# Expert values: 88 of 128 blocks gathered by row, 40 read in order and multiplied by a one-hot weight matrix; all key rows first

## The chip, the cores and the metric

The kernel runs on one core of a Trainium2 chip. The metric is the time of one execution on the device in microseconds. The profile shows the engines PE (TensorE), DVE (VectorE), ACT (ScalarE), POOL (GpSimd) and SP (SyncE), and the 16 DMA engines that all of them use.

## The reference, cut to what matters

Two transformer blocks run over 256 tokens of width 2048. Everything up to the second block's mixer is left out here: the change does not touch it. The last layer is a product-key expert layer:

```python
q = (xt @ wq).reshape(T, 8, 2, 128)
s1 = einsum('thd,nd->thn', q[:, :, 0], subkeys[0])
s2 = einsum('thd,nd->thn', q[:, :, 1], subkeys[1])
v1, i1 = top_k(s1, 16)
v2, i2 = top_k(s2, 16)
cand = (v1[..., :, None] + v2[..., None, :]).reshape(T, 8, 256)
sc, ci = top_k(cand, 16)
e1 = take_along_axis(i1, ci // 16, axis=-1)
e2 = take_along_axis(i2, ci % 16, axis=-1)
idx = e1 * 128 + e2
gate = softmax(sc, axis=-1)
h = gelu(einsum('cd,chkd->chk', xc, u[idx]))
out = einsum('chk,chkd->cd', gate * h, v[idx])
```

Each token picks 16 experts in each of 8 heads, 128 picks in all. An expert has a row of `u` and a row of `v`, each 2048 f32 numbers (8 KB). There are 16384 experts: 128 blocks (by `e1`) of 128 rows (by `e2`), 1 MB a block. The result is added to x, and a last RMS norm with a gain gives the output.

## The kernel before, in words

The 256 tokens are two tiles of 128, one token per partition. The picks of one head for one tile are a group `g` of 16 (tile `g // 8`, head `g % 8`); there are 16 groups. POOL fetches rows by indirect DMA, `gather` (L620): one DMA brings, for pick `r` of group `g`, one row per partition, 128 rows of 8 KB. Eight slots of 1 MB in SBUF (four in `arena`, four in `proj`) take the rows in turn: row number n goes to slot `n % 8`, and POOL waits until the slot's earlier row was used (`free0` to `free7`). The order is 16 u rows of group 0, and from then on one u row of group `g + 1` and one v row of group `g` in turn (`U_ROW`, `V_ROW`).

DVE does the choosing and the dot products. `choose_sides` takes the best 16 of each side's 128 scores, `choose_sums` the best 16 of the 256 sums, and `experts_of` (L2670) turns them into row numbers. `dot_row` (L2712) multiplies a u row with x and sums. ACT's gelu and DVE's `weigh` (L2729) make the 16 weights of a group. Three of four v rows are added by PE: ACT makes a diagonal matrix of the weights (L1068) and PE multiplies it with the row, four matmuls of 512 columns into PSUM (L1899). The others are added by DVE: `add_row` (L2722) is one SCALAR_TENSOR_TENSOR over 2048 columns, then a wait for itself and a semaphore raised for the slot. `link` is a helper that raises DVE's own semaphore and waits for it.

In between PE still works out the queries of heads 4 to 7 (`ask_part`, L1873), for which SP loads blocks of `peer_wq`; ACT copies their scores out (`take_head`). SP then loads the final gain (L399, a broadcast load of 128 rows of 8 KB). `join` (L2744) adds PE's sums to x and `last_mean` and `last_norm` do the final norm: for tile 0 at groups 8 to 10, beside the gathers of tile 1, and for tile 1 at the end. ACT takes the squares' sums (L1012) and roots (L1014), and writes half of tile 1's output.

## Time and profile before

| | |
|---|---|
| median of 3 runs | 3221.64 us (3220.44 to 3223.31) |
| span of the profiled execution | 3220.0 us |
| busy, share of the span | PE 84%, DVE 62%, POOL 29%, ACT 14% |
| DMA | 922.82 MB, mean 287 GB/s |
| expert stage in the span | from 1890.84 us on |

The span runs from the first to the last instruction of the profiled execution. No time of its own is listed for that execution outside the profile; the median of the runs is 1.6 us above its span, and that is taken for what lies around it. Busy shares are means over stages with different limits, so the stage that the change touches is read by itself.

### The profile page before, as it was taken

To read this page: it belongs to the slowest core of one execution; us is meant where nothing else is said; L and a number is where in the kernel's file an instruction comes from. 1 tells how busy PE (TensorE), PEld (TensorE's weight loads), DVE (VectorE), ACT (ScalarE), POOL (GpSimd) and SP (SyncE) were. 2 spreads that over 40 slices of the span, in tenths; PEclk is the share of its full clock that TensorE was granted. 3 is DMA by queue.
4 is the path that set the end of the run, shared out by engine and by line. 5 is a ranking of instruction groups with operands and counts; after the bars stand their busy time and mean duration, and the time that the engine had idled before them with its cause. 6 is when DMAs were issued, how large, how long until landed. Compare 5 with 4: busy or idle time off the path is not lost.

```text
span 3220.0 us, 26360 instructions
## 1 busy us (share of the span) xinstructions
PE 2717.7 (84%) x9138; PEld 1612.9 (50%) x9138; DVE 1985.4 (62%) x3009; ACT 441.8 (14%) x1072; POOL 926.9 (29%) x713
## 2 busy tenths in 40 slices
PE   5999998999999999999999996878666666666666
PEld 2444666488888884445568473434322222222222
DVE  6555466288666655543037668667766676776655
ACT  1000133211111010002037021000000001000001
POOL 2111200000000000000014036556566566666664
PEclk9999989999999999999999997889887888888888
DMA  9999541467555545555440569999999999999998
GB/s 377 359 397 399 201 134 40 170 222 256 162 169 169 169 157 183 174 179 164 131 157 1 198 254 417 419 419 422 422 422 421 422 414 400 422 422 422 422 422 355
DMA packets 250245, 922.82 MB, mean 287 GB/s; under 512 B 16732, under 2 KB 44580, under 8 KB 183844
## 3 DMA queue, kind: packets, MB, share of 16 engines
q0 software_dynamic: 99840, 637.57, 48.3%
q1 hardware_dynamic: 149893, 283.38, 26.4%
q8 instruction: 54, 0.88, 0.1%
q10 hardware_dynamic: 416, 0.66, 0.1%
q14 instruction: 42, 0.34, 0.0%
HBM read 918.35 MB, written 8.44 MB: 288 GB/s over the span
## 4 chain that ended last, share of the span: by engine, by line
PE 56%; DMA 22%; DVE 11%; POOL 5%; issue 4%; ACT 2%; POOLq 0%; SPq 0%; DVEq 0%; ACTq 0%
PE ps L1505 16%; DMA arena<-in_peer_v,proj 13%; PE ps L1133 12%; PE ps L1551 8%; PE ps L1899 7%; DMA proj<-in_peer_v,proj 5%; PE ps L1749 3%; DMA arena<-in_peer_u,proj 3%; POOL proj L625 3%; DMA arena<-in_w_mod 2%; PE ps L1175 2%; PE ps L1259 1%; DVE arena L2716 1%; PE ps L1272 1%; DVE proj L2716 1%
## 5 line engine op out<-in xcount | busy, mean ns | idle before, releaser
L1899 PE MATMUL ps<-arena,gates 128*128 128x512 f32 x516 | 364.9, 872 | 368.9 <-DMA arena<-in_peer_v,proj 255.1
L1899 PE MATMUL ps<-proj,gates 128*128 128x512 f32 x992 | 449.4, 598 | 39.2 <-DMA proj<-in_peer_v,proj 38.9
L1899 PEld LDWEIGHTS ps<-arena,gates 128*128 128x128 f32 x516 | 142.0, 289 | 585.0 <-issue 455.4
L2716 DVE CUSTOM_DVE_ANT_0 proj<-proj,yT 128x2048 f32<-128x2048 f32 x128 | 291.8, 2291 | 229.5 <-DMA proj<-in_peer_u,proj 228.9
L1133 PE MATMUL ps<-ring,hT 128*128 128x512 f32 (+3 forms) x960 | 373.5, 551 | 1.8 <-DVE arena L2427 1.8
L2716 DVE CUSTOM_DVE_ANT_0 arena<-arena,yT 128x2048 f32<-128x2048 f32 x128 | 292.3, 2292 | 119.9 <-DMA arena<-in_peer_u,proj 116.4
L1899 PEld LDWEIGHTS ps<-proj,gates 128*128 128x128 f32 x992 | 184.7, 190 | 289.0 <-issue 287.8
L1133 PEld LDWEIGHTS ps<-ring,hT 128*128 128x128 f32 x960 | 180.1, 192 | 191.9 <-issue 165.6
L625 POOL DMA_INDIRECT arena<-in_peer_u,proj x128 | 200.1, 1563 | 234.2 <-PE ps L1817 119.2
L625 POOL DMA_INDIRECT proj<-in_peer_u,proj x128 | 230.0, 1797 | 100.2 <-DVE proj L2716 57.2
L1505 PE MATMUL ps<-arena,yT 128*128 128x256 f32 x1056 | 242.3, 379 | 0.0
L595 POOL COPY proj<-proj 128x256 f32 (+1 forms) x16 | 5.9, 395 | 814.5 <-DVE proj L2481 814.5
L625 POOL DMA_INDIRECT proj<-in_peer_v,proj x128 | 188.1, 1470 | 135.0 <-PE ps L1899 117.3
L625 POOL DMA_INDIRECT arena<-in_peer_v,proj x128 | 172.3, 1346 | 160.9 <-PE ps L1899 135.6
L1505 PEld LDWEIGHTS ps<-arena,yT 128*128 128x128 f32 x1056 | 199.0, 190 | 26.2
L1969 DVE SCALAR_TENSOR_TENSOR arena<-arena,c_col 128x1024 f32<-128x1024 f32 (+1 forms) x120 | 154.2, 1285 | 76.4 <-DMA arena<-in_w_mod 73.8
L1505 PE MATMUL ps<-ring,hT 128*128 128x256 f32 x704 | 166.4, 379 | 1.2 <-ACT hT L665 1.2
L2725 DVE SCALAR_TENSOR_TENSOR x<-arena,proj,x 128x2048 f32<-128x2048 f32 x63 | 148.1, 2350 | 15.4 <-DMA arena<-in_peer_v,proj 15.4
L2315 DVE TENSOR_TENSOR arena<-ring 128x512 f32<-128x512 f32 x88 | 60.9, 692 | 148.3 <-PE ps L1505 147.9
L1505 PEld LDWEIGHTS ps<-ring,hT 128*128 128x128 f32 x704 | 133.7, 190 | 19.9 <-ACT hT L665 1.4
L542 POOL DMA_DIRECT2D arena<-in_w_mod x80 | 56.8, 710 | 280.9 <-PE ps L1133 129.2
L591 POOL DMA_DIRECT2D proj<-in_w_mod x16 | 11.3, 708 | 384.4 <-DVE gates L1969 200.2
(500 smaller groups left out, 3727.9 us busy)
## 6 DMA issues: line engine op xcount, KB each, us to landing
arena<-in_w_mod POOLq DMA_DIRECT2D x80, 1024.0 KB
ring<-in_ffn_w_gate SPq DMA_DIRECT2D x44, 1024.0 KB, 5.2
ring<-in_ffn_w_up SPq DMA_DIRECT2D x44, 1024.0 KB, 5.2
ring<-in_ffn_w_down SPq DMA_DIRECT2D x88, 512.0 KB, 5.2
ring<-in_w_in SPq DMA_DIRECT2D x40, 1024.0 KB, 8.7
ring<-in_w_out SPq DMA_DIRECT2D x16, 1024.0 KB, 5.2
proj<-in_w_mod POOLq DMA_DIRECT2D x16, 1024.0 KB
ring<-in_w_out SPq DMA_DIRECT2D x32, 512.0 KB, 4.8
```

Of the source, the lines that this page charges most:

```text
L542: pool_eng.dma_start(mod["ring"][:, j % 4], w_mod[:, 2 * j:2 * j + 2, cols]).then_inc(sem(f"mod_slot{j % 4}"), 16)
L625: pool_eng.indirect_dma_start(row_slots[n % ROWS], None, table, bass.IndirectOffsetOnAxis(expert[:, 0, TOP * g + r:TOP * g + r + 1], 0))\
L1133: ins = pe.matmul(ps[:, 2 * (b % 2) + t, 0:w], lhs[:, KS * (order[s] if between and b == 0 else s) + k, P * t:P * (t + 1)], ring[:, s, k, ...
L1175: ins = pe.matmul(ps[:, 2 * b + t, 0:FIRST], hT[:, KS * q + k, P * t:P * (t + 1)], ring[:, b, k, 0:FIRST], start=(q == 0 and k == 0), stop ...
L1505: ins = pe.matmul(up_ps(m, UP_PLACE[name], 1), tokens(j), weights[:, j, :], start=first and name in UP_FIRST, stop=(q == SLOTS - 1 and j = ...
L1551: return pe.matmul(ps[:, bank[name], :], lhs, rhs, start=(k == 0), stop=(k == HALF_K - 1))
L1749: return pe.matmul(ps[:, bank[name], :], lhs, rhs, start=(k == 0), stop=(k == OUT2_HALF - 1))
L1899: ins = pe.matmul(ps[:, 4 * t + b, :], diag[:, j, :], row_slots[n % ROWS][:, NB * b:NB * (b + 1)], start=(h == 0 and j == 0), stop=(h == H ...
L1969: ins = vec.scalar_tensor_tensor(out=to, in0=w, scalar=c, in1=to, op0=ALU.mult, op1=ALU.add)
L2315: link(vec.tensor_tensor(w["S1"], a21, a22, ALU.add), "w_sums", wait=False)
L2716: vec.tensor_tensor_reduce(slot, slot, xs[:, g // HEADS], 1.0, 0.0, ALU.mult, ALU.add, peer["h16"][:, 0, r:r + 1]).then_inc(sem(f"free{n % ...
L2725: link(vec.scalar_tensor_tensor(out=x[:, t], in0=row_slots[n % ROWS], scalar=peer["weight"][:, 0, TOP * g + r:TOP * g + r + 1], in1=x[:, t ...
```

## The change

The value blocks 88 to 127 (`TILES = 40`) are no longer gathered. Their rows are read in order, a block of 128 rows at a time, and multiplied on PE by a weight matrix [128 experts of the block, 128 tokens] for each block and tile. The gathers of v get a bound (`bounds_check=LAST_GATHERED`): rows past block 87 are skipped, the slot keeps what it held, and the weight for them is set to 0 (`near`).

The reference, run on its own inputs, puts 29.9% of tile 0's picks and 31.4% of tile 1's into these 40 blocks.

The weight matrices are built from one-hot rows. ACT and PE turn the picks (`side1` = e1, `side2` = e2, and the weights) so that one column holds the 128 picks of a token. For four tokens at a time (`GROUP`), DVE compares e2 with 0..127 (`hot2`, 4 x 128 columns) and e1 with 88..127 (`hot1`, 4 x 40 columns), POOL multiplies `hot1` by the weights, PE multiplies the two (one matmul of 40 columns per token), and ACT copies the result into `W_HOME`. A tile takes 32 such steps.

The order changes. All u rows go first; tile 0's 128 v rows are mixed in from group 2 on, 9 to a group of 16 u rows, and PE adds all of them. Tile 0's weight matrices are built beside groups 9 to 14. After the last u row come tile 1's 128 v rows, all of them added by DVE. Tile 1's weight matrices are built first, four steps ahead of each of DVE's first eight additions. SP loads the first three blocks once all experts are known; the other 37, and the final gain ahead of them, wait until all weight matrices are built and then for PE's release of a buffer of three. Tile 0's `join` and norm move to the end, ahead of tile 1's. The final gain moves into `arena`; `vrows` and `vcols` become one tensor; the table of constants gets 128 columns of iota for 16.

```diff
+    U_ORDER = [(g, r) for g in range(GS) for r in range(TOP)]
+    V_AFTER = {}
+    for g in range(2, GS):
+        for r in range(TOP):
+            if (9 * r) // TOP != (9 * (r + 1)) // TOP or (g >= GS - 2 and r == 0):
+                V_AFTER[g, r] = len(V_AFTER)
+    assert len(V_AFTER) == PICKS
+    U_ROW, V_ROW = {}, {}
+    for g, r in U_ORDER:
+        U_ROW[g, r] = len(U_ROW) + len(V_ROW)
+        if (g, r) in V_AFTER:
+            V_ROW[V_AFTER[g, r]] = len(U_ROW) + len(V_ROW)
+    for v in range(PICKS, 2 * PICKS):
+        V_ROW[v] = 2 * PICKS + v
...
+    TILES = 40
+    GATHERED = P - TILES
+    LAST_GATHERED = P * GATHERED - 1
+    GROUP = 4
+    GROUPS = P // GROUP
+    SPREAD_AT = {TOP * (HEADS + 1) + 3 * i: i for i in range(GROUPS)}
+    PE_LAG, POOL_LAG = 4, 8
+    TAIL = 4
+    spread_at = lambda g, r, lag=0: SPREAD_AT.get(TOP * g + r - lag)
+    HOT = GROUP * (P + TILES)
...
+    v_tiles = (tab[:, TAB.shape[1] - D:], gates[:, 0, :], arena[:, D:2 * D])
+    NV = len(v_tiles)
+    v_in = lambda e: at(f"slot{e % NV}", 16 * (BLK["wq"] + 3 + e // NV + 1))
+    v_used = lambda n: at("unit_used", SLOTS * (BLK["wq"] + 4) + n)
...
-        sp.wait_ge(*at("unit_used", SLOTS * (BLK["wq"] + 4)))
-        load("norm_in", out_gain, a["final_norm_2"].partition_broadcast(P))
+        sp.wait_ge(*at("experts", GS + 1))
+        for e in range(TILES):
+            if e == NV:
+                sp.wait_ge(*at("w_built", 2 * GROUPS))
+                load("norm_in", out_gain, a["final_norm_2"].partition_broadcast(P))
+            if e >= NV:
+                sp.wait_ge(*v_used(e - NV + 1))
+            sp.dma_start(v_tiles[e % NV], a["peer_v_2"][P * (GATHERED + e):P * (GATHERED + e + 1), :]).then_inc(sem(f"slot{e % NV}"), 16)
...
+        def gather_v(v):
+            n = V_ROW[v]
+            row_wait(n)
+            pool_eng.indirect_dma_start(row_slots[n % ROWS], None, a["peer_v_2"], bass.IndirectOffsetOnAxis(expert[:, 0, v:v + 1], 0),
+                                        bounds_check=LAST_GATHERED, oob_is_err=False).then_inc(sem(f"row{n % ROWS}"), 16)
+        def hot_weights(i):
+            t, j = divmod(i, GROUPS)
+            pool_eng.wait_ge(*at("pick_out", 3 if t else 1))
+            pool_eng.wait_ge(*at("hot", i + 1))
+            pool_eng.tensor_tensor(hot1(i), hot1(i), pick_T(t, 2)[:, GROUP * j:GROUP * (j + 1)].unsqueeze(2).to_broadcast([P, GROUP, TILES]), ALU.mult)\
+                    .then_inc(sem("hot_weights"), 1)
...
+        for g, r in U_ORDER:
+            if g == 0 and r % FEW == 0:
                 pool_eng.wait_ge(*at("experts", r // FEW + 1))
+            if g and r == 0:
+                pool_eng.wait_ge(*at("experts", g + 2))
+            gather_u(g, r)
+            if (g, r) in V_AFTER:
+                gather_v(V_AFTER[g, r])
+            if spread_at(g, r, POOL_LAG) is not None:
+                hot_weights(spread_at(g, r, POOL_LAG))
+        for v in range(PICKS):
+            for i in range(TAIL * (v - ROWS), TAIL * (v - ROWS + 1)):
+                if 0 <= i < GROUPS:
+                    hot_weights(GROUPS + i)
+            gather_v(PICKS + v)
...
+        def diag_out(v):
+            act.wait_ge(*at("weights", v // TOP + 1))
+            if v >= NDIAG:
+                act.wait_ge(*row_free(V_ROW[v - NDIAG]))
+            act.activation(diag[:, v % NDIAG, :], ident, ACT.Copy, scale=peer["near"][:, 0, v:v + 1]).then_inc(sem("diag_out"), 1)
+        def picks_out(n, lo, hi):
+            act.wait_ge(*at("pick_turned", n + 1))
+            t = min(n, 1)
+            act.copy(vboth[:, 3 * t + lo:3 * t + hi, :], ps[:, 6, P * lo:P * hi].rearrange("p (k m) -> p k m", m=P)).then_inc(sem("pick_out"), 1)
+        def spread_out(i):
+            t, j = divmod(i, GROUPS)
+            act.wait_ge(*at("w_built", i + 1))
+            built = ps[:, w_bank(i), 0:GROUP * TILES].rearrange("p (j e) -> p e j", j=GROUP)
+            for lo, n, home in W_HOME[t]:
+                ins = act.copy(home[:, :, GROUP * j:GROUP * (j + 1)], built[:, lo:lo + n, :])
+            ins.then_inc(sem("w_out"), 1)
...
+        def add_row(v):
+            n = V_ROW[v]
+            pe.wait_ge(*at("diag_out", v + 1))
+            pe.wait_ge(*row_in(n))
+            for b in range(SLOTS):
+                ins = pe.matmul(ps[:, b, :], diag[:, v % NDIAG, :], row_slots[n % ROWS][:, NB * b:NB * (b + 1)], start=(v == 0), stop=False, skip_group_check=True)
+            ins.then_inc(sem(f"free{n % ROWS}"), 1)
...
+        def spread(i):
+            pe.wait_ge(*at("hot_weights", i + 1))
+            if i >= 2:
+                pe.wait_ge(*at("w_out", i - 1))
+            for j in range(GROUP):
+                ins = pe.matmul(ps[:, w_bank(i), TILES * j:TILES * (j + 1)], hot2(i)[:, j, :], hot1(i)[:, j, :], start=True, stop=True)
+            ins.then_inc(sem("w_built"), 1)
...
+        def sum_values(t, e, banks):
+            pe.wait_ge(*v_in(e))
+            for b in banks:
+                ins = pe.matmul(ps[:, 4 * t + b, :], spread_weights(t, e), v_tiles[e % NV][:, NB * b:NB * (b + 1)],
+                                start=(t == 1 and e == 0), stop=(e == TILES - 1), skip_group_check=True)
+            return ins
+        pe.wait_ge(*at("weights", GS))
+        turn_picks(1, (2,))
+        for i in range(GROUPS):
+            spread(GROUPS + i)
+            early = i - (GROUPS - SLOTS * NV)
+            if early >= 0:
+                sum_values(0, early // SLOTS, (early % SLOTS,))
+        pe.wait_ge(*at("w_out", 2 * GROUPS))
+        for e in range(TILES - NV):
+            if e >= NV:
+                sum_values(0, e, range(SLOTS))
+            sum_values(1, e, range(SLOTS)).then_inc(sem("unit_used"), 1)
+        for t, banks in ((0, range(SLOTS)), (1, (2, 3)), (1, (0, 1))):
+            for e in range(TILES - NV, TILES):
+                ins = sum_values(t, e, banks)
+            ins.then_inc(sem("values_done"), 1)
...
-        def add_row(g, r):
-            t, n = g // HEADS, V_ROW(g, r)
+        def add_row(v):
+            n = V_ROW[v]
             vec.wait_ge(*row_in(n))
-            link(vec.scalar_tensor_tensor(out=x[:, t], in0=row_slots[n % ROWS], scalar=peer["weight"][:, 0, TOP * g + r:TOP * g + r + 1], in1=x[:, t],
-                                          op0=ALU.mult, op1=ALU.add))
+            link(vec.scalar_tensor_tensor(out=x[:, 1], in0=row_slots[n % ROWS], scalar=peer["near"][:, 0, v:v + 1], in1=x[:, 1], op0=ALU.mult, op1=ALU.add))
             vec.sem_inc(sem(f"free{n % ROWS}"), 1)
+        def hot_sides(i):
+            t, j = divmod(i, GROUPS)
+            vec.wait_ge(*at("pick_out", t + 1))
+            if i >= 3:
+                vec.wait_ge(*at("w_built", i - 2))
+            place = lambda k, n: pick_T(t, k)[:, GROUP * j:GROUP * (j + 1)].unsqueeze(2).to_broadcast([P, GROUP, n])
+            vec.tensor_tensor(hot2(i), place(1, P), tb("iota").unsqueeze(1).to_broadcast([P, GROUP, P]), ALU.is_equal)
+            vec.tensor_tensor(hot1(i), place(0, TILES), tb("iota")[:, GATHERED:P].unsqueeze(1).to_broadcast([P, GROUP, TILES]), ALU.is_equal).then_inc(sem("hot"), 1)
...
+            link(vec.scalar_tensor_tensor(out=w, in0=w, scalar=total, in1=peer["h"][:, 0, TOP * g:TOP * (g + 1)], op0=ALU.mult, op1=ALU.mult))
+            picks = slice(TOP * g, TOP * (g + 1))
+            link(vec.scalar_tensor_tensor(out=peer["near"][:, 0, picks], in0=peer["side1"][:, 0, picks], scalar=float(GATHERED), in1=w, op0=ALU.is_lt, op1=ALU.mult), "weights")
...
+            if 0 < g < GS - 1:
+                choose_sides(g + 1)
             for r in range(TOP):
+                dot_row(g, r)
+                if (g, r) == (0, 3):
+                    choose_sides(1)
+                if r == (3 if g else 7) and g + 1 < GS:
+                    choose_sums(g + 1)
+                if g and r == 5:
+                    weigh(g - 1)
+                if spread_at(g, r) is not None:
+                    hot_sides(spread_at(g, r))
+            dots_done(g)
+        for i in range(GROUPS, GROUPS + 2):
+            hot_sides(i)
+        weigh(GS - 1)
+        for v in range(PICKS):
+            for i in range(TAIL * v, TAIL * (v + 1)):
+                if 2 <= i < GROUPS:
+                    hot_sides(GROUPS + i)
+            add_row(PICKS + v)
+        join(0)
+        last_mean(0)
+        last_norm(0)
```

## Rows read from the trace of the kernel before

**Rows 1.** The page's 40 slices (part 2), and POOL's first gather in the timeline.

```profile
DMA  9999541467555545555440569999999999999998
...
1890.84 1.04 POOL L625 DMA_INDIRECT arena<-in_peer_u,proj  x1 [119.17 <-PE ps L1817]
```

**Rows 2.** Windows of 80 us; x counts instructions; then clock, DMA share, rate.

```profile
core 0: us, PE busy (x) PEld busy (x) DVE busy (x) ACT busy (x) POOL busy (x), PEclk, DMA share, GB/s
...
2520.00:2600.00 80.00, 51.37 (x96) 20.62 (x94) 55.98 (x78) 6.79 (x17) 47.54 (x33) 0.83 1.01 421
...
2680.00:2760.00 80.00, 51.04 (x95) 20.82 (x94) 55.60 (x78) 10.45 (x23) 50.75 (x33) 0.83 0.98 401
```

**Rows 3.** The page's costliest groups: busy us, mean ns, idle before and its releaser.

```profile
L2716 DVE CUSTOM_DVE_ANT_0 proj<-proj,yT 128x2048 f32<-128x2048 f32 x128 | 291.8, 2291 | 229.5 <-DMA proj<-in_peer_u,proj 228.9
...
L2725 DVE SCALAR_TENSOR_TENSOR x<-arena,proj,x 128x2048 f32<-128x2048 f32 x63 | 148.1, 2350 | 15.4 <-DMA arena<-in_peer_v,proj 15.4
```

**Rows 4.** DVE's timeline at the end: start, duration, instruction, idle before.

```profile
3188.14 2.35 DVE L2725 SCALAR_TENSOR_TENSOR x<-arena,proj,x 128x2048 f32<-128x2048 f32 x1 [2.62 <-DMA arena<-in_peer_v,proj]
3193.11 2.35 DVE L2725 SCALAR_TENSOR_TENSOR x<-arena,proj,x 128x2048 f32<-128x2048 f32 x1 [2.62 <-DMA arena<-in_peer_v,proj]
...
3207.98 1.28 DVE L2741 SCALAR_TENSOR_TENSOR x<-arena,proj,x 128x1024 f32<-128x1024 f32 x1 [2.57 <-DMA arena<-in_peer_v,proj]
```

**Rows 5.** DVE's timeline: choosing sides and weighing; choosing sums, then dots in a row.

```profile
1954.11 0.17 DVE L2720 COPY proj<-proj 128x16 f32<-128x16 f32 x1
...
1958.02 2.29 DVE L2716 CUSTOM_DVE_ANT_0 arena<-arena,yT 128x2048 f32<-128x2048 f32 x1
...
1980.42 0.42 DVE L2707 TENSOR_TENSOR arena<-arena 128x256 f32<-128x256 f32 x1
...
1987.64 2.29 DVE L2716 CUSTOM_DVE_ANT_0 proj<-proj,yT 128x2048 f32<-128x2048 f32 x1
...
1989.86 2.29 DVE L2716 CUSTOM_DVE_ANT_0 proj<-proj,yT 128x2048 f32<-128x2048 f32 x1
```

**Rows 6.** DVE's two-input operations over 512 and 256 columns.

```profile
L2315 DVE TENSOR_TENSOR arena<-ring 128x512 f32<-128x512 f32 x88 | 60.9, 692 | 148.3 <-PE ps L1505 147.9
...
L2678 DVE TENSOR_TENSOR arena<-arena,tab 128x256 f32<-128x256 f32 x32 | 13.7, 427 | 1.1
```

**Rows 7.** DVE's timeline where such an operation raises a semaphore for another engine.

```profile
1905.43 2.35 DVE L2771 SCALAR_TENSOR_TENSOR yT<-x,stat,arena 128x2048 f32<-128x2048 f32 x1
1907.98 2.29 DVE L2716 CUSTOM_DVE_ANT_0 arena<-arena,yT 128x2048 f32<-128x2048 f32 x1 [0.19 <-DVE yT L2771]
```

**Rows 8.** DMA queues while the final gain loads, 2284 to 2286 us.

```profile
q1 hardware_dynamic: 58, 0.48, 56.8%
q0 software_dynamic: 52, 0.37, 44.4%
```

**Rows 9.** PE among the last gathers: eight matmuls, and the window around them.

```profile
3190.74 3.67 PE L1899 MATMUL ps<-arena,gates 128*128 128x512 f32 x8 [1.30 <-DMA arena<-in_peer_v,proj]
...
3190.00:3200.00 10.00, 7.34 (x16) 2.88 (x16) 4.76 (x3) 0.00 (x0) 2.25 (x2) 1.00 1.01 420
```

**Rows 10.** DVE's timeline from the first join of the end to its last product.

```profile
3209.41 1.22 DVE L2749 TENSOR_TENSOR x<-x,ps 128x1024 f32<-128x1024 f32 x1
...
3214.54 1.28 DVE L2763 SCALAR_TENSOR_TENSOR x<-x,stat,hT 128x1024 f32<-128x1024 f32 x1
```

**Rows 11.** POOL's timeline beside dots in a row and beside idle; window of the whole stage.

```profile
1944.13 1.91 POOL L625 DMA_INDIRECT arena<-in_peer_u,proj  x1 [0.31 <-issue]
1946.34 1.91 POOL L625 DMA_INDIRECT proj<-in_peer_v,proj  x1 [0.30 <-issue]
...
1976.71 0.94 POOL L625 DMA_INDIRECT proj<-in_peer_u,proj  x1 [0.30 <-issue]
1977.96 0.94 POOL L625 DMA_INDIRECT arena<-in_peer_v,proj  x1 [0.30 <-issue]
...
1890.00:3210.00 1320.00, 910.20 (x2109) 424.36 (x2108) 916.08 (x1260) 123.17 (x310) 790.50 (x512) 0.84 1.00 415
```

More of the change, by code:

```diff
@@ L619, in _, with row_wait @@
         head_pair(0, 7, False)
-        def gather(table, g, r, n):
+        def row_wait(n):
             pool_eng.wait_ge(*at(f"free{n % ROWS}", n // ROWS + 1))
@@ L624, in gather, with gather_u @@
                 pool_eng.wait_ge(*at("unit_used", SLOTS * BLK["wq"] + n - 2))
-            pool_eng.indirect_dma_start(row_slots[n % ROWS], None, table, bass.IndirectOffsetOnAxis(expert[:, 0, TOP * g + r:TOP * g + r + 1], 0))\
+        def gather_u(g, r):
+            n = U_ROW[g, r]
+            row_wait(n)
+            pool_eng.indirect_dma_start(row_slots[n % ROWS], None, a["peer_u_2"], bass.IndirectOffsetOnAxis(expert[:, 0, TOP * g + r:TOP * g + r + 1], 0))\
                     .then_inc(sem(f"row{n % ROWS}"), 16)
-        for r in range(TOP):
-            if r % FEW == 0:
-                pool_eng.wait_ge(*at("experts", r // FEW + 1))
-            gather(a["peer_u_2"], 0, r, U_ROW(0, r))
@@ L632, in _ @@
[L632 to L638 removed]
+        def gather_v(v):
+            n = V_ROW[v]
+            row_wait(n)
+            pool_eng.indirect_dma_start(row_slots[n % ROWS], None, a["peer_v_2"], bass.IndirectOffsetOnAxis(expert[:, 0, v:v + 1], 0),
+                                        bounds_check=LAST_GATHERED, oob_is_err=False).then_inc(sem(f"row{n % ROWS}"), 16)
@@ L1033, in take_head, with take_scores @@
             act.copy(peer["q"][:, h % 2], ps[:, pair:pair + 2, 0:T]).then_inc(sem("wq_out"), 1)
+        def take_scores(h):
+            pair = 4 + 2 * (h % 2)
             act.wait_ge(*at("keys_scored", h + 3))
@@ L1057, in _ @@
         for h in range(2, EARLY):
-            take_head(h)
-        best_exp(1)
-        for g in range(GS):
-            act.wait_ge(*at("h_done", g + 1))
-            h = peer["h"][:, 0, TOP * g:TOP * (g + 1)]
-            act.activation(h, h, ACT.Gelu_apprx_tanh).then_inc(sem("h_gelu"), 1)
-            act.wait_ge(*at("weights", g + 1))
-            if g:
-                act.wait_ge(*v_added(g - 1))
-            for j, r in enumerate(by_pe(g)):
-                act.activation(diag[:, j, :], ident, ACT.Copy, scale=peer["weight"][:, 0, TOP * g + r:TOP * g + r + 1]).then_inc(sem("diag_out"), 1)
-            if g == HEADS + 1:
-                last_norm(0)
-            if 0 < g <= HEADS - EARLY:
-                take_head(EARLY + g - 1)
-            if g + 2 < GS:
-                best_exp(g + 2)
+            take_queries(h)
+            take_scores(h)
+        for g, r in U_ORDER:
+            if g and r == 0:
+                row_gelu(g - 1)
+            if (g, r) in V_AFTER:
+                diag_out(V_AFTER[g, r])
+            if (g, r) in TAKE_Q:
+                take_queries(TAKE_Q[g, r])
+            if (g, r) in TAKE_SCORES:
+                take_scores(TAKE_SCORES[g, r])
+            if r == 9 and g + 1 < GS:
+                best_exp(g + 1)
+            if (g, r) == (HEADS, 8):
+                picks_out(0, 0, 3)
+            if (g, r) == (GS - 1, 8):
+                picks_out(1, 0, 2)
+            if spread_at(g, r, PE_LAG) is not None:
+                spread_out(spread_at(g, r, PE_LAG))
+        row_gelu(GS - 1)
+        picks_out(2, 2, 3)
+        for i in range(GROUPS, 2 * GROUPS):
+            spread_out(i)
         act.activation(stat[:, 12:13], stat[:, 30:31], ACT.Sqrt)
+        last_norm(0)
         last_norm(1)
@@ L1887, in _ @@
         score_head(EARLY - 1)
-        for g in range(GS):
-            t, h = g // HEADS, g % HEADS
-            if g == HEADS:
+        def add_row(v):
[5 more added lines that the diff above has]
+            ins.then_inc(sem(f"free{n % ROWS}"), 1)
@@ new lines, in turn_picks @@
+        def turn_picks(t, ks):
+            for k in ks:
+                src = peer[("side1", "side2", "weight")[k]][:, 0, PICKS * t:PICKS * (t + 1)]
+                ins = pe.transpose(ps[:, 6, P * k:P * (k + 1)], src, ident)
+            ins.then_inc(sem("pick_turned"), 1)
+        def spread(i):
[5 more added lines that the diff above has]
+            ins.then_inc(sem("w_built"), 1)
@@ new lines, in _ @@
+                pe.wait_ge(*at("weights", HEADS))
+                turn_picks(0, range(3))
+            if (g, r) == (GS - 1, 8):
+                pe.wait_ge(*at("experts", GS + 1))
+                pe.wait_ge(*at("pick_out", 1))
+                turn_picks(1, range(2))
+            if spread_at(g, r, PE_LAG) is not None:
+                spread(spread_at(g, r, PE_LAG))
+        def sum_values(t, e, banks):
[4 more added lines that the diff above has]
+            return ins
```

140 lines of the change are left out of this document (52 added, 88 removed).

## The prediction

> **What bounds the kernel now.** I read the forty slices of the page first, to find the stage. From slice 25 on the DMA row is full [rows 1]: this is the expert stage, from 1890.8 us, where the first gather is issued, to 3208 us, where the last one lands [rows 1, 4]. Busy time in a window of 80 us, one group's time, shows the DMA at 1.01 of 16 engines and 421 GB/s while DVE is busy for 56 us, PE for 51 and POOL for 48 [rows 2]. So transfers set the pace, and DVE has 24 us in 80 to spare. The groups by line say the same: the dot products' idle time ends on DMA, 229.5 us of it before one of the two groups [rows 3]. The pace itself stands at the end of the timeline: DVE takes every second row there and starts a new one each 4.97 us [rows 4], so one gather of 128 rows of 8 KB costs 2.485 us. 512 of them are 1272 us of the 1317.
>
> **What the change removes.** The reference's own picks, counted, lie in the last 40 blocks for 29.9% of tile 0 and for 31.4% of tile 1. If a skipped row costs nothing, a value gather falls to 0.701 x 2.485 = 1.74 us (tile 0) and 0.686 x 2.485 = 1.70 us (tile 1): 95 + 100 = 195 us of DMA go, and 40 blocks of 1 MB, 99 us, come back. Net 96 us of transfers. The question is how much of that reaches the end, since u rows now come first and DVE alone adds tile 1 (128 additions where it had 67, one of them half a row).
>
> **Stage 1, all u rows and tile 0's values.** Groups 0 and 1 have no values. A group costs DVE 16 dots at a pitch of 2.22 us, 35.5, choosing sides and weighing 3.9, choosing sums 7.2 [rows 5], and the new masked weights, about 0.2, by the other operations of 16 columns (0.17 [rows 5]): 47 us, against 40 of transfers, so DVE sets these two. From group 2 a group moves 16 u rows and 9.14 value rows, 39.8 + 15.9 = 55.7 us, which is above DVE's 47 and, with 5.33 pairs of one-hot compares from group 9 on, above 53. A pair is 512 and 160 columns: 0.69 and 0.33 us, between the rows for 512 and 256 columns [rows 6]. PE's 36 matmuls per group are 16 us at the pitch below: hidden. ACT's diagonals too. The end of the stage, worked out from before: the last landing, 3208, less 128 tile-1 gathers (318), less tile 0's skipped rows (95), less the gain load and tile 0's output (5), less about 8 us by which the windows of the stage fell short of 422 GB/s, half of them in the one where tile 0 was joined, normed and written out (401 GB/s) [rows 2], plus three value blocks that SP loads early (7.5): 2789. **Stage 1 ends at 2797.**
>
> A rule of the Trainium skill bears on the second: DMA: Bandwidth & Descriptors, section The descriptor swizzle, ties four and four partitions to an engine. By it the busiest engine would hold 772 rows and the stage would end 17 us later than even skipping gives; no row here shows which engine a row used.
>
> **Stage 2, the second weight matrix.** DVE's last weights go through ACT, PE and POOL: about 6 us. Then DVE alternates four pairs of compares, 4 x 1.05, with one addition, eight times. An addition is 2.35 us [rows 3] and waits for itself and raises a semaphore; the same pattern left 0.2 us before the next instruction [rows 7], so 2.55. With some waits for POOL and PE, three deep, I take 7.3 a turn, 58 in all; bounds 6.75 (no wait) and 9 (one POOL operation per turn held up by an addition). Together **64 us, to 2861**. Until then only the first three blocks can be loaded, and only eight gathers refill: DMA idles for about half, some 30 us, of what was saved.
>
> **Stage 3, the blocks.** SP's queue then brings 37 blocks and the gain while POOL's brings gathers. The only load of this form beside a full gather queue, the final gain, got 58 packets where the gathers got 52 in the two microseconds in which it ran throughout [rows 8], so each side gets half, and a block takes 4.97 us. PE needs 8 matmuls per block, 3.67 us, and that very rhythm, 8 per 4.97 us, ran at a clock of 1.00, the 2.4 GHz level [rows 9], so PE keeps up and three buffers keep SP's queue full. 38 x 4.97 = **189 us, to 3050**. A gather now takes 2 x 1.70 = 3.41 us, so 55 land, and DVE, which could do 74, starves.
>
> **Stage 4, what is left.** Of 128 rows 8 were added, 8 had landed, 55 came: 57 remain at DVE's 2.55 (their transfers, 1.70, are shorter): **145 us, to 3195**. The order of the two queues thus costs what the skipping gained: first DVE waits for DMA, then DMA for DVE.
>
> **The end.** Before, 10.6 us passed from the first join to the end of the span [rows 10]. Tile 0's join, norm and output were hidden; they now stand ahead of it on DVE: two joins of 1.22, squares and root 2.5, two products of 1.28: 7.6. In all 18 us, **3213**. The profile's span is 3220.0, the median of the runs 3221.6, so 1.6 lies around it: **3215 us**, 0.2% less.
>
> **The rivals.** *DVE stays fed (faster).* If SP's loads get less than half, say 40%, stage 3 takes 38 x 2.485 / 0.4 = 236 us, gathers take 2.84 us, 83 land, 29 remain: 236 + 74 = 310 where the sum has 334, so 3191; with no starving at all DVE's 120 additions, 306, give 3187. For it: a block waits for PE's release, a gather only for DVE. Against: the packets of the gain load.
>
> *POOL becomes the bound (slower).* Where DVE works without a gap, POOL issues one gather per dot, 2.21 us apart; where DVE runs short operations or idles, 1.25 us apart [rows 11]. Stage 1 asks 25.1 gathers and, from group 9 to 14, 5.33 products of a group that should take 55.7 us. That is 1.83 us each: from there this decides, and the mean of the whole stage before was 1.54 + 0.30 = 1.84 (512 gathers in 790 us, and the gap named issue) with DVE busy for some 70% [rows 11]. It will be 85 to 95%. At 2.05 those six groups take 62 us, 38 more, so 3253; at 2.21, 69 more. A bounds check that lengthens the gather adds to it. Against: when DMA sets the pace DVE waits for rows, and in these gaps POOL is fast.
>
> The Trainium skill speaks for this one: GPSIMD Engine Reference, section Key points, says that POOL shares its SBUF interfaces with VectorE and contends with instructions that have two SBUF inputs, as the dots have; the pitch of 2.21 agrees, and by that rule the compares and additions would hold POOL up too.
>
> *Skipping saves nothing (slower).* If a row out of bounds is fetched from a clamped address, stage 1 is 95 us longer; in stage 3 a gather takes 4.97, 38 land, 74 remain, 189 us instead of 145: 3215 + 95 + 44 = 3354. Nothing in this trace speaks for or against, as no gather had a bound; it is the plainest way for the change to fail.
>
> **How the numbers follow.** A measurement here tells 0.2% (6.4 us) from no change. The sum holds with chance 0.52; its own bounds, about -20 (no additions, 6.75 a turn) to +35, spread it as 0.23 faster, 0.15 same, 0.14 slower, likeliest range 3195 to 3250. DVE fed: 0.20, faster. POOL: 0.22, of which 0.20 slower and 0.02 same. No saving: 0.06, slower. Together faster 0.43, same 0.17, slower 0.40. Both signs hold much, because four engines come within some per cent of each other once DMA gives way. The range, 3178 to 3270, takes in the fed case below and most of POOL's above, and leaves out the clamped one.
>
> **What would show it.** Right: some 880 MB moved instead of 923; the last dot near 2800; POOL's product and PE's small matmuls between 2797 and 2861 with DMA half idle; additions 3.4 us apart to 3050 and 2.55 after it; DVE, not DMA, in the chain at the end. Wrong: fewer than 40 MB saved (clamping); groups 9 to 14 over 58 us with POOL busy throughout (its rival); additions evenly 2.55 apart while blocks land (the fed case); a PE clock of 0.5 (1.2 GHz) among the blocks, which would make 8 matmuls 6.9 us and PE the bound.

## The result, and the profile after

The changed kernel takes 3304.8 us (median of 4 runs, 3297.7 to 3309.9), the kernel before 3222.5 (4 runs, 3220.4 to 3223.4): 1.0255 times as long (95% interval 1.0240 to 1.0269). The forecast of 3215 was 90 us short, and its range ended at 3270. The profiled execution took 3304.8 us with a span of 3303.1.

The page of the changed kernel: the slices, and the queue of the gathers.

```profile
DMA  9999530476545445544513599999999889939996
...
DMA packets 256018, 882.74 MB, mean 267 GB/s; under 512 B 27416, under 2 KB 55264, under 8 KB 194528
...
q0 software_dynamic: 99840, 555.32, 42.4%
```

Skipping works: 883 MB are moved instead of 923, as forecast. The packets of the gathers' queue are as many as ever; a skipped row shows as a small packet ("under 512 B": 27416, before 16732). But in the slices the DMA row, full in [rows 1], now has two eights late in stage 1 and, behind two more nines, a 3: that is stage 2, where little can be fetched.

Where the stages end is read from DVE: the copy behind a group's last dot (its line over the whole span, then three in the timeline), and the additions of tile 1, whose last begins at 3283.3.

```profile
L2875 DVE COPY proj<-proj x16: 174/174/418, 1956.1 to 2881.2; 128x16 f32<-128x16 f32 x16
L2880 DVE SCALAR_TENSOR_TENSOR x<-arena,proj,x x64: 2344/2351/2353, 2889.2 to 3283.3; 128x2048 f32<-128x2048 f32 x64
```

```profile
2065.40 0.17 DVE L2875 COPY proj<-proj 128x16 f32<-128x16 f32 x1
2412.71 0.17 DVE L2875 COPY proj<-proj 128x16 f32<-128x16 f32 x1
2881.15 0.17 DVE L2875 COPY proj<-proj 128x16 f32<-128x16 f32 x1
```

Stage 1 ends at 2881 instead of 2797: 84 of the 90 us are lost there. Group 1, from 1956.1 to 2002.9, took the 47 us of the forecast. Groups 3 to 8 took (2412.7 - 2065.4) / 6 = 57.9 us each instead of 55.7, and groups 9 to 15 (2881.2 - 2412.7) / 7 = 66.9. Behind stage 1 the sum held: 404 us to the last addition's end at 3285.6 (forecast 398) and 17.5 to the end of the span (18).

Windows of the changed kernel, columns as in [rows 2]: among groups 4 to 7, among groups 10 to 13, and among the blocks.

```profile
2120.00:2360.00 240.00, 174.19 (x372) 75.80 (x370) 195.48 (x323) 26.16 (x65) 182.43 (x104) 0.89 0.99 405
2500.00:2740.00 240.00, 172.83 (x409) 82.85 (x408) 183.53 (x289) 27.36 (x88) 161.29 (x109) 0.81 0.91 351
...
3000.00:3080.00 80.00, 80.00 (x188) 35.41 (x187) 66.09 (x29) 0.00 (x0) 57.92 (x29) 1.00 1.00 404
```

Two losses show. In groups 10 to 13 DMA stands idle for 9% of the time, yet no engine is full: DVE 76%, POOL 67%, PE 72%. In groups 4 to 7 DMA is full by its share but moves 405 GB/s, where a full stretch of [rows 2] had 421. So first: what does an idle DMA wait for, if every engine has time?

The waits of 2500 to 2740 (who waited for whom: us in all, times, longest):

```profile
...
PE ps L2015 <- POOL arena L690: 46.9, 17, 6.2
DVE proj L2871 <- DMA proj<-in_peer_u,proj: 31.9, 15, 9.4
POOL proj L682 <- PE ps L1999: 22.7, 6, 6.4
...
POOL arena L682 <- PE ps L1999: 20.6, 5, 6.7
...
PE ps L1999 <- ACT gates L1121: 17.3, 19, 2.4
```

It is a circle: PE waits for POOL's product (L690), POOL for a slot that PE's addition (L1999) frees, and DVE for the rows that POOL could not ask for. The timeline of one turn, from POOL, PE and DVE:

```profile
2609.68 2.99 POOL L682 DMA_INDIRECT proj<-in_peer_v,proj  x1 [5.90 <-PE ps L1999]
2612.97 0.95 POOL L676 DMA_INDIRECT proj<-in_peer_u,proj  x1 [0.30 <-issue]
2613.95 0.46 POOL L690 TENSOR_TENSOR arena<-arena,vboth 128x160 f32<-128x160 f32 x1
...
2614.46 1.40 PE L2015 MATMUL ps<-arena 128*128 128x40 f32 x8 [2.15 <-POOL arena L690]
2616.60 6.32 PE L1999 MATMUL ps<-arena,gates 128*128 128x512 f32 x8 [0.74 <-ACT gates L1121]
2622.76 3.60 PE L1999 MATMUL ps<-proj,gates 128*128 128x512 f32 x8
...
2621.14 2.29 DVE L2871 CUSTOM_DVE_ANT_0 proj<-proj,yT 128x2048 f32<-128x2048 f32 x1 [9.36 <-DMA proj<-in_peer_u,proj]
```

POOL's product is short, but it stands in POOL's queue behind two gathers, and the first of these waited 5.90 us for a slot. PE's small matmuls wait for the product, ACT's next diagonal (L1121) stands behind its copy of their result, and PE's next addition, which frees the next slot, behind that diagonal. That addition then runs 6.32 us where its neighbour takes 3.60: the granted clock was 0.58 from 2616.6 to 2622.9 and 1.00 in the 3.5 us behind, so PE ran most of it at the 1.2 GHz level, after waits of 2.15 and 0.74 us. Over the whole window the clock was 0.81, against 0.89 in groups 4 to 7. Meanwhile DVE has no row for 9.36 us.

### The profile page after: what moved, and what is told of

It is laid out like the page before. It is cut to its first block, busy times and chain, and to the rows that moved or that the text cites. A ratio compares the mean times of both kernels' runs of the same rounds, so it can differ in the third digit from the quotient of the medians.

```text
span 3303.1 us, 28590 instructions
## 1 busy us (share of the span) xinstructions
PE 2873.1 (87%) x9812; PEld 1737.8 (53%) x9812; DVE 2191.4 (66%) x3213; ACT 443.8 (13%) x1109; POOL 1118.8 (34%) x777
## 2 busy tenths in 40 slices
DMA packets 256018, 882.74 MB, mean 267 GB/s; under 512 B 27416, under 2 KB 55264, under 8 KB 194528
## 4 chain that ended last, share of the span: by engine, by line
PE 54%; DVE 13%; DMA 11%; POOL 11%; issue 9%; ACT 2%; POOLq 0%; DVEq 0%; SPq 0%; ACTq 0%
PE ps L1611 16%; PE ps L1239 11%; PE ps L1657 8%; DMA arena<-in_peer_v,proj 4%; PE ps L1281 3%; DMA proj<-in_peer_u,proj 3%; PE ps L1999 3%; PE ps L1855 3%; POOL proj L682 2%; POOL arena L682 2%; POOL arena L676 2%; DVE x L2880 2%; POOL proj L676 2%; DVE proj L2871 2%; DVE arena L2871 2%
## 5 line engine op out<-in xcount | busy, mean ns | idle before, releaser
L1999 PE MATMUL ps<-proj,gates 128*128 128x512 f32 x504 | 287.0, 725 | 88.3 <-DMA proj<-in_peer_v,proj 71.0
L1999 PE MATMUL ps<-arena,gates 128*128 128x512 f32 x520 | 279.4, 689 | 87.8 <-DMA arena<-in_peer_v,proj 52.1
L682 POOL DMA_INDIRECT arena<-in_peer_v,proj x129 | 249.1, 1931 | 100.5 <-PE ps L1999 40.4
L1239 PEld LDWEIGHTS ps<-ring,hT 128*128 128x128 f32 x960 | 179.4, 191 | 191.1 <-issue 164.1
L682 POOL DMA_INDIRECT proj<-in_peer_v,proj x127 | 227.6, 1792 | 98.8 <-PE ps L1999 48.7
L1999 PEld LDWEIGHTS ps<-proj,gates 128*128 128x128 f32 x504 | 113.5, 234 | 244.0 <-issue 219.9
L1999 PEld LDWEIGHTS ps<-arena,gates 128*128 128x128 f32 x520 | 111.0, 221 | 237.6 <-issue 196.2
L2015 PE MATMUL ps<-arena 128*128 128x40 f32 x512 | 100.1, 366 | 83.6 <-POOL arena L690 83.1
L2880 DVE SCALAR_TENSOR_TENSOR x<-arena,proj,x 128x2048 f32<-128x2048 f32 x64 | 150.5, 2351 | 23.7 <-DMA arena<-in_peer_v,proj 17.5
L2880 DVE SCALAR_TENSOR_TENSOR x<-proj,x 128x2048 f32<-128x2048 f32 x64 | 150.5, 2352 | 22.5 <-DMA proj<-in_peer_v,proj 15.7
L2015 PEld LDWEIGHTS ps<-arena 128*128 128x128 f32 x512 | 96.5, 280 | 123.5 <-POOL arena L690 112.1
```

Of the source, the lines that this page charges most:

```text
L682: pool_eng.indirect_dma_start(row_slots[n % ROWS], None, a["peer_v_2"], bass.IndirectOffsetOnAxis(expert[:, 0, v:v + 1], 0), bounds_check= ...
L1239: ins = pe.matmul(ps[:, 2 * (b % 2) + t, 0:w], lhs[:, KS * (order[s] if between and b == 0 else s) + k, P * t:P * (t + 1)], ring[:, s, k, ...
L1999: ins = pe.matmul(ps[:, b, :], diag[:, v % NDIAG, :], row_slots[n % ROWS][:, NB * b:NB * (b + 1)], start=(v == 0), stop=False, skip_group_ ...
L2015: ins = pe.matmul(ps[:, w_bank(i), TILES * j:TILES * (j + 1)], hot2(i)[:, j, :], hot1(i)[:, j, :], start=True, stop=True)
L2880: link(vec.scalar_tensor_tensor(out=x[:, 1], in0=row_slots[n % ROWS], scalar=peer["near"][:, 0, v:v + 1], in1=x[:, 1], op0=ALU.mult, op1=A ...
```

## The experiments

The first four runs were to tell three theories apart: the circle; POOL's rate; and the bound itself, if it makes gathers dearer than what skipping saves. Each is one profiled run beside one of the kernel before (3222.1 to 3224.1 in these). "Last dot" is the last copy behind a group; "groups 3 to 8" is the mean, read like the one above. What single runs can tell apart shows where two of them do the same up to the last dot: 2881.2 and 2886.1 (the changed kernel, and the run with three blocks), 2832.1 and 2833.9 (products on DVE, and the run with a changed tail). Counted from the end of group 2, either pair differs by 4 us, and so smaller differences of such times say nothing.

### The circle of waits

**No building beside the gathers** (tile 0's weight matrices aren't built, so the blocks' part of tile 0 is left out):

```diff
-    SPREAD_AT = {TOP * (HEADS + 1) + 3 * i: i for i in range(GROUPS)}
+    SPREAD_AT = {}
```

> Left out: the building of tile 0's weight matrices beside groups 9 to 14 (compares, products, small matmuls, copies), so tile 0's block sums multiply stale numbers; the 40 blocks are still read and multiplied. Theory A (ring): groups 9 to 15, 67 us each in the changed kernel, are held by a ring of in-order waits: POOL's product stands behind gathers eight places ahead, PE's small matmuls wait for it, PE's value rows and ACT's diagonals stand behind these and keep the slots that POOL's next gathers need. Without the building they fall to the 58 us of groups 2 to 8: seven times 9 is 63 us less, about 3240. Theory B (POOL's rate): POOL cannot issue so many operations beside a busy DVE: the same 3240, since five products a group go. Theory C (the skipped rows still cost transfer time): the building is not it, groups 9 to 15 stay near 67, about 3300.

3255.1 us; last dot 2831.1, 50 us earlier. Groups 9 to 15 took 59.6 us; the time is 15 us over the 3240 expected, in part because group 14, in which SP loads three blocks, still took 67.5.

**PE's small matmuls seven rows behind the compares instead of four**, with nothing left out:

```diff
-    PE_LAG, POOL_LAG = 4, 8
+    PE_LAG, POOL_LAG = 7, 8
```

> Only PE_LAG 4 to 7: PE's small matmuls and ACT's copies stand three value positions later in their queues; every operation stays. Theory A: PE no longer waits for the product, so the ring opens: groups 9 to 15 near 60 us, about 3255. Theory B: POOL's operations and their rate are the same, so groups 9 to 15 stay at 66 to 68 and the time at 3300 within 6. Theory C: also 3300.

3259.6 us; last dot 2835.0. Its window of 2500 to 2740:

```profile
2500.00:2740.00 240.00, 176.14 (x460) 83.81 (x458) 208.27 (x343) 29.35 (x96) 199.70 (x124) 0.89 0.99 394
```

POOL has the same instructions, even more of them in this window (x124 for x109) and is busier (200 us for 161), yet the last dot comes 46 us earlier and DMA is full. So not POOL's rate but the place of the wait cost the time.

**Tile 0's products on DVE**, which multiplies the one-hot rows right behind the compares:

```diff
+            if t == 0:
+                link(ins)
+                ins = vec.tensor_tensor(hot1(i), hot1(i), place(2, TILES), ALU.mult)
...
-            if spread_at(g, r, POOL_LAG) is not None:
-                hot_weights(spread_at(g, r, POOL_LAG))
```

> Tile 0's 32 products move from POOL to DVE, one more 160-column operation (about 0.35 us with its wait) per step; the tail is as it was. Theory A: the product no longer stands behind gathers, so the ring opens though PE_LAG is 4: groups 9 to 15 near 60, about 3255. Theory B: POOL is relieved of 5.33 operations of 1.0 + 0.3 us a group, 7 us: groups 9 to 14 near 60, about 3260. Theory C: about 3310, since DVE gets 13 us more in all. With the lag run: both faster is A, this alone is B, neither is C.

3256.2 us; last dot 2832.1, as without the building. The line of its last dots, and its window of 2500 to 2740:

```profile
L2873 DVE COPY proj<-proj x16: 174/174/205, 1957.9 to 2832.1; 128x16 f32<-128x16 f32 x16
...
2500.00:2740.00 240.00, 172.12 (x470) 83.08 (x470) 217.06 (x375) 31.97 (x103) 175.46 (x106) 0.92 0.99 406
```

Once the circle is open, the building thus costs no more than these runs can tell: either of its two links, POOL's place or PE's, opens it, and **some 49 us** were its price. The clock rose with it, from 0.81 to 0.92; how much of the 49 us the lower clock was, no run separates.

### What skipping is worth

**All rows fetched** (no bound; the weights of the blocks' rows stay 0):

```diff
-                                        bounds_check=LAST_GATHERED, oob_is_err=False).then_inc
+                                        ).then_inc
```

> The gathers of v have no bound: all 128 rows come, the weights of those past block 87 stay 0, so the result is the same. If skipping frees the transfer (A and B): 38 rows of tile 0 are 95 us more DMA; groups 2 to 8 rise from 58 to about 62.5, groups 9 to 15 have DMA to spare (its share is 0.9 there) and rise by 0 to 3; the tail's 128 gathers and 38 other loads are 412 us of transfers where it took 404, so 20 to 40 more. About 3365, between 3340 and 3400; 923 + 42 MB. If skipped rows cost what full ones do (C): 3300 within 6.

3372.2 us; last dot 2894.0, groups 3 to 8 61.8 us. Without the bound DMA moves 426 GB/s in 2120 to 2360. So 29.9% of the value rows skipped saved (61.8 - 57.9) / 9.14 = 0.43 us per gather, where the forecast took 0.745. One expectation failed: groups 9 to 15 did not rise by 0 to 3 us, they fell from 66.9 to 65.2, with the building and its circle in place and 411 GB/s moved in 2500 to 2740. The run with short dots below, without bound and circle, took 63.9 there, so here the circle cost at most some 9 us of seven groups: its price isn't fixed, and why it fell no run shows.

**The kernel before with the bound alone** (no blocks; a skipped row adds what the slot held):

```diff
-                gather(a["peer_v_2"], g, r, V_ROW(g, r))
+                gather(a["peer_v_2"], g, r, V_ROW(g, r), bounds_check=P * 88 - 1, oob_is_err=False)
```

> The kernel before with the bound on its value gathers alone: no blocks are read, and a skipped row's place in the sum is taken by what the slot held (the values of blocks 88 to 127 are left out). What skipping is worth by itself, in a stage that DMA sets throughout. If a skipped row costs nothing, as the prediction had it: 128 x 0.745 + 128 x 0.78 = 195 us less, 3029. If a gather saves only what the first experiments suggest, (61.7 - 57.8) / 9.14 = 0.42 us: 256 x 0.42 = 108 us less, 3116. If POOL's pace sets it: a pair of gathers cannot take less than POOL's 2 x 2.21, which is 4.42 of 4.97 us, 141 us less, 3083.

3112.2 us: 110 saved, 0.43 per gather again, in another order of the work and again at a rate below the full one (389 GB/s at a DMA share of 0.98 in 2120 to 2360). The next five runs all have the products on DVE, so that the circle is out of the way, and ask where the rest goes: POOL, the skipped rows themselves, or their uneven lot.

**An even 25%** (tile 0's value gathers take fixed rows; its values are not the reference's), and **the same 25% in partitions 0 to 31**:

```diff
+    skip = ((i + i // 16) % 4 == 3)[:, None] & (np.arange(P) >= 0)[None, :]
+    cols["fixed"] = np.where(skip, P * P - 1, take).astype(np.int32).view(np.float32)
```

```diff
-    skip = ((i + i // 16) % 4 == 3)[:, None] & (np.arange(P) >= 0)[None, :]
+    skip = (i < 32)[:, None] & (np.arange(P) >= 0)[None, :]
```

> The run with tile 0's products on DVE, and in it tile 0's value gathers take fixed rows from a constant table: in every group of four partitions, and in every group of eight, one of four rows is out of bounds (25%), the rest lie spread over blocks 0 to 87. Tile 0's values are therefore not the reference's. Without any skipping a group of 16 u rows and 9.14 value rows took 61.7 us (median of groups 3 to 8 of the run without bounds); with the real picks, 29.9% skipped, 57.5 us. If skipped rows cost nothing but lie unevenly over the DMA engines, an even 25% saves 9.14 x 0.25 x 2.485 = 5.7 us: groups 3 to 8 take 56.0 us, less than with 29.9%, and the last dot product ends at about 2812. If it is not the unevenness, and a skipped row costs some 0.4 of a fetched one wherever it lies, 25% saves 9.14 x 0.25 x 2.485 x 0.6 = 3.4 us: groups of 58.3 us, the last dot product at about 2843.

> As the run with an even 25% skipped, but the rows out of bounds are those of partitions 0 to 31 in every one of tile 0's value gathers (tile 0's values are not the reference's). If a DMA engine serves fixed partitions, the engines that serve the others save little or nothing: groups 3 to 8 take between 60 and 61.7 us, and the DMA's mean busy share falls below 0.97. If the rows of a gather are dealt out to whichever engine is free, or in turns of one partition, it is as the even run.

The even run: 3245.6 us, last dot 2820.4, groups 3 to 8 57.4. Partitions 0 to 31: 3305.6 us, last dot 2881.9, groups 3 to 8 61.7. Their windows, the even run first:

```profile
2120.00:2360.00 240.00, 170.63 (x372) 75.04 (x372) 195.04 (x325) 26.17 (x65) 192.53 (x106) 0.91 1.01 415
```

```profile
2120.00:2360.00 240.00, 174.12 (x365) 76.61 (x364) 182.39 (x297) 27.01 (x64) 144.19 (x97) 0.87 0.96 386
```

The second is plain: the same number of skipped rows saves nothing when they lie in 32 partitions, and DMA's share falls to 0.96. So what moves a row hangs on its partition, and whatever has the most rows to move sets the pace. That these are the DMA engines is the plainest reading, though no row names the engine of a packet; a dealing in turns of single partitions is out. The first came out between its two cases: POOL was busy for 192.5 us and between instructions (106 times 0.3) for some 32 more, so POOL may have become the limit there, and nothing could be read of the rows.

**Dots over 1024 of 2048 columns** take POOL and DVE out of it (h and the weights are then not the reference's): with the real picks, with the even 25%, and without a bound.

```diff
-            vec.tensor_tensor_reduce(slot, slot, xs[:, g // HEADS], 1.0, ...
+            vec.tensor_tensor_reduce(slot[:, 0:D // 2], slot[:, 0:D // 2], xs[:, g // HEADS, 0:D // 2], 1.0, ...
```

> The run with tile 0's products on DVE, and the dot products over the first 1024 of the 2048 columns (h, and so every weight, is not the reference's; the picks and the rows that move stay the same). [...] In the run with whole dots groups 3 to 8 took 57.5 us while POOL was at work or between two instructions for 220 of 240 us. If POOL's pace held that stage above the predicted 55.7, groups 3 to 8 fall to 61.7 - 9.14 x 0.299 x 2.45 = 55.0 us, and the last dot product ends near 2800. If the uneven lot of the DMA engines holds it, they stay between 56.4 and 57.4 us (the busiest engine of each stretch, worked out from the reference's picks with some four to eight gathers on the way), and it ends between 2815 and 2832.

> The run with an even 25% of rows out of bounds (fixed rows for tile 0's values, which are not the reference's), and the dot products over 1024 columns. With whole dots its groups 3 to 8 took 57.4 us, but POOL was at work or between two instructions for 232 of 240 us. If that was POOL's pace, groups fall to 61.7 - 9.14 x 0.25 x 2.45 = 56.1 us and the 8 KB packets come without gaps at 420 GB/s or more. If each skipped row costs time in the DMA engines, they stay at 57 or above.

> The run with short dots without any bound: every row is fetched (skipped blocks count with weight 0, h from 1024 columns). The pace of DMA alone, for the two runs above to be taken from: with whole dots 61.7 us a group. If DMA set that, it stays at 61.4 to 61.9; if POOL or DVE had a part in it, it falls below 61.

Windows of the three, in this order:

```profile
2120.00:2360.00 240.00, 171.28 (x381) 75.69 (x380) 131.57 (x334) 23.20 (x58) 118.26 (x105) 0.92 1.00 414
```

```profile
2120.00:2360.00 240.00, 178.51 (x376) 77.93 (x376) 129.66 (x327) 23.21 (x58) 116.52 (x105) 0.88 1.01 425
```

```profile
2120.00:2360.00 240.00, 170.50 (x354) 74.29 (x353) 117.63 (x297) 24.49 (x59) 104.07 (x97) 0.86 1.01 426
```

| run | groups 3 to 8 | last dot | from group 2's last dot to there |
|---|---|---|---|
| whole dots, products on DVE | 57.6 | 2832.1 | 764.9 |
| short dots, real picks | 56.5 | 2809.2 | 756.1 |
| short dots, even 25% | 56.6 | 2803.2 | 748.2 |
| short dots, no bound | 61.8 | 2878.0 | 817.9 |

With DMA alone in charge a gather costs 61.8 / 25.14 = 2.46 us, and 119 value gathers lie behind group 2. An even 25% should save 119 x 0.25 x 2.46 = 73 us of 817.9 and leave 744.7; it left 748.2, at 425 GB/s. So **an evenly skipped row is all but free**: 3.5 us of 73, which such runs can't tell from nothing (a group took 56.6 us, between its two cases and nearer to the free one). The real 29.9% should save 87.5 and leave 730.4; it left 756.1. Of these 25.7 us, 3.5 go like those of the even run, and **22 are put down to uneven lots**, by exclusion: POOL and DVE have time, and the same picks without a bound move 426 GB/s, so it isn't the addresses. The 56.5 us lie where the estimate from the picks had them, 56.4 to 57.4. Whole dots add 764.9 - 756.1 = **9 us, POOL and DVE** together. Groups 0 and 1, which DVE sets and which short dots shorten by some 15 us, are left out of these differences; they are also why the last dot of the run with real picks came earlier than expected.

### The tail

**Only the first 3 of the 40 blocks** (the other 37 blocks' part of the output is left out):

```diff
-        for e in range(TILES):
+        for e in range(NV):
```

> The changed kernel with only the first 3 of the 40 blocks read and multiplied (37 blocks' part of the output is left out). Stage 1 stays at 2881. If DVE's additions set the end and the blocks take few turns from them, the last addition ends 120 x 2.5 = 300 us after the eighth one, at 2881 + 76 + 300 = 3257, and the total is about 3276, 29 us less than the changed kernel. If the blocks on PE set the end, or gathers starve beside them as the prediction had it (55 rows at 3.4 us), the total falls by 50 us or more.

3282.1 us, 22.7 less. The last dot came at 2886.1 (5 later, in a stage that the edit doesn't touch), the last addition began at 3260.6, and from the eighth on they ran at 2.5 us without a gap:

```profile
L2873 DVE SCALAR_TENSOR_TENSOR x<-arena,proj,x x64: 2342/2351/2353, 2895.0 to 3260.6; 128x2048 f32<-128x2048 f32 x64
```

So the end is DVE's additions, and the 37 blocks cost it 328 - 300 = 28 us of waits for rows, no more.

**Tile 1's compares beside sixteen additions** instead of eight, on top of the products on DVE:

```diff
-    TAIL = 4
+    TAIL = 2
```

> The run with tile 0's products on DVE, and tile 1's compares spread over sixteen additions, two pairs ahead of each, where there were four pairs ahead of each of eight. If the turns of 7.7 and 13.7 us were waits for the ring of three pairs of one-hot rows (compares 4 x 1.05 and one addition 2.5 make 6.7 without a wait), the waits hide behind the extra additions: sixteen turns of some 4.7 us, 75 in all for sixteen additions, where 76 us held eight, and the end comes 8 x 2.5 = 20 us earlier, at 3236. If PE's queue of matrices and blocks sets the end, it moves by less than 5 us.

3247.5 us, 8.7 less than without it; from the last dot to the last addition's end it is 394.4 us for 404.9, 10.5 less, half of what was expected. DVE's waits for PE behind the last dot fell from 24.3 us (20 times, changed kernel) to 11.7 (8 times):

```profile
DVE arena L2888 <- PE ps L2013: 11.7, 8, 3.6
```

Most turns took 4.8 us, as expected, but the last four 5.1 to 6.8, and with the compares spread out the last pair ended 10 us later behind the last dot. This is the fastest version here that leaves nothing out, still 0.7% above the kernel before.

## Why the prediction was wrong

**The stage and its limit: right.** Stage 1 is set by gathers, group 1 took DVE's 47 us, and 883 MB are moved.

**The building beside groups 9 to 14, put down as hidden: this step failed, and by the most.** The forecast weighed each engine's busy time against 55.7 us a group ("hidden. ACT's diagonals too", compares up to DVE's 53, the products a part of "POOL's pace, taken as 3") and gave the waits between engines no term at all. It did not follow in what order the engines wait for one another. The building ties POOL's queue to PE's and both to the slots: POOL's product stands eight u rows, with their value gathers some 12 gathers, beyond its compares, but there are only eight slots, so POOL gets there only as PE frees slots; and PE's small matmuls, four rows beyond the compares, hold up the very additions that free them. Worked out: a u row with its share of values is 1.57 gathers, eight slots are 5.1 rows, so for the product at row 8 the slots of row 2.9 must be free, and PE stands at row 4: one row of slack. Three more opened it. Price some 49 us. PE also had less room than the forecast thought: by the rows below a 512-column matmul is two records, so the 36 matmuls of a group are 72 records, 33 us at the 3.67 for eight and not 16, and PE was busy for 72% of the window. The POOL rival forecast a time in that direction (62 us a group, 3253) by another mechanism, and its own sign, POOL busy throughout, was missing: 161 of 240 us.

**"Uneven skipping, taken as 3": mis-sized.** What is left for it is 22 us, about the bound of 20. The prefetch doesn't even it out: in the run with products on DVE a gather landed some 11 us after its issue (median) where one was issued each 2.3 us, so four or five are on their way, and each is done only when its fullest share has landed. The Trainium skill (DMA: Bandwidth & Descriptors, section The descriptor swizzle) ties fixed groups of four partitions to an engine. The run that skips partitions 0 to 31 (61.7 us a group, as without a bound) agrees that an engine serves fixed partitions; which engine serves which, no run here shows. The 17 us that the prediction worked out by that rule, an estimate, were nearer than the 3 that was taken.

**"POOL's pace, taken as 3"**: POOL and whole dots on DVE together cost 9 us. In the run with products on DVE, POOL was at work (183 us) or between instructions (106 times 0.3) for some 215 of 240 us in 2120 to 2360 and else waited for slots, so its share of the 9 stays open. Without its three additions the forecast had 2789 for the last dot; it came 92 us later. Of these, 49 + 26 + 9 = 84 are measured, one change after the other; in another order they would share out differently, as the run without a bound shows. The other 8 stay open; group 2, at 62.5 us in most runs with whole dots, may hold some of them.

**Stage 2: 64 us, measured 76.** The rule of alternating held, but the last two turns took 13.7 us, not 7.3. The timeline there shows PE putting two records of the early blocks between its small matmuls, and DVE, three pairs ahead at most, waiting for each:

```profile
2929.85 2.06 PE L2041 MATMUL ps<-tab,hT 128*128 128x512 f32 x2
2931.70 1.77 PE L2015 MATMUL ps<-arena 128*128 128x40 f32 x8
...
2933.57 0.69 DVE L2890 TENSOR_TENSOR arena<-vboth,tab 128x512 f32<-128x512 f32 x1 [2.44 <-PE ps L2015]
```

**Stage 3, "8 matmuls per block, 3.67 us": wrong by a factor of two.** The row with x8 in [rows 9] is one value row, which the code adds with four matmuls: a 512-column f32 matmul is two records. A block takes eight matmuls, so two such rows:

```profile
3001.30 3.60 PE L2041 MATMUL ps<-tab,hT 128*128 128x512 f32 x8
3004.74 3.60 PE L2041 MATMUL ps<-tab,ring 128*128 128x512 f32 x8
3008.18 3.59 PE L2041 MATMUL ps<-gates,hT 128*128 128x512 f32 x8
```

From one block's tab row to the next buffer's are 6.88 us, PE is busy for 80 of 80 us at a clock of 1.00, and the blocks last until 3237 instead of 3050. PE was the bound there at the 2.4 GHz level, which the prediction expected only of the 1.2 GHz one. PE's release, not an even split of the queues, now times SP's loads; the gathers' queue moved 48.4 MB to the loads' 29.2 in 2990 to 3180, and DVE is nearly fed:

```profile
3028.38 2.35 DVE L2880 SCALAR_TENSOR_TENSOR x<-arena,proj,x 128x2048 f32<-128x2048 f32 x1 [1.00 <-DMA arena<-in_peer_v,proj]
3031.13 4.85 DVE L2880 SCALAR_TENSOR_TENSOR x<-arena,proj,x 128x2048 f32<-128x2048 f32 x2 [0.41 <-DMA arena<-in_peer_v,proj]
...
3046.68 9.85 DVE L2880 SCALAR_TENSOR_TENSOR x<-arena,proj,x 128x2048 f32<-128x2048 f32 x4
```

While the blocks last, gaps of 0.4 to 2.3 us stand before some 30 of the additions, which else follow each other each 2.5 us, not the even 3.4 us that was forecast. The rival in which DVE stays fed thus described the tail better; 120 additions took 328 us, against 334 in the sum and 306 in the rival, so the sum came out by luck: two errors cancel.

**The range** left out 3305 because each bounded addition was bounded by an engine's rate alone. Without the circle (3256) the result would have been in it, on the slower side. Its lower bound, "about -20", adds up to -12 (8 for no additions, eight turns of 0.55), which bears on nothing here.

**What is left of the idea.** The bound alone saves 110 us in the old order. The forecast priced the 40 blocks at 99 us of DMA, from [rows 4]; that leaves some 11 for building two tiles' matrices and a longer end. No version run here that leaves nothing out beats the kernel before.

## What to carry to other kernels

Before calling work hidden because each engine has idle time, write down for each queue what stands ahead of its wait and who frees that: a step shared by three engines that also share a ring of buffers needs slack in rows, not in busy time. Rows skipped in a gather are worth only what the least relieved set of partitions saves, so count them by partition and not by their mean. And check what a record counts (a row of x8 against the loops of the code) before multiplying it.

## What the runs showed of the hardware

- Skipped rows cost next to nothing by themselves (3.5 us for some 3,800 of them, each still a small packet of the queue), but where they all lie in partitions 0 to 31 they also save nothing: 61.7 us a group, 61.8 without a bound.
- DMA's busy share hides most of this loss: in 2120 to 2360, 0.99 to 1.00 at 405 to 414 GB/s with real picks, where the even and the unbounded run with short dots moved 425 and 426 at 1.01. The rate tells it better than the share.
- POOL was busy for 117 and 118 us of 240 beside short dots and for 183 and 193 beside whole ones, for the same 105 or 106 gathers, and without a bound for 104 and 144, for 97; a single one takes 0.95 to 2.99 us in the timeline above, as [rows 11] had 0.94 and 1.91. The Trainium skill (GPSIMD Engine Reference, section Key points) says that POOL contends with two-input instructions of VectorE; the halved dots agree.
